# Staging the next expert's weights in dead attention buffers, with Pool copying them home, in a mixture-of-experts kernel

## Chip, cores and metric

The kernel runs on 1 core of one Trainium2 chip. The metric is the device time of one execution in microseconds (us); before the change the median of 3 runs is 1287.46 us (1286.85 to 1291.06).

The engines by their short names: PE is TensorE, DVE is VectorE, ACT is ScalarE, POOL is GpSimd, SP is SyncE, which here only issues DMAs.

## What is computed

One layer (float32, 256 latent tokens, 256 context tokens, width 1024): neighbourhood attention, a residual, then a mixture of experts over the 256 latent tokens, each token going to 4 of 32 experts. The experts' weights are 32 x (8 + 4) MiB = 403 MB and are read once.

```python
def moe(x, w_router, b_router, w_up, b_up, w_down, b_down):
    logits = (xt @ w_router + b_router).astype(jnp.float32)
    top_v, top_i = lax.top_k(logits, TOP_K)
    top_w = jax.nn.softmax(top_v, axis=-1)
    gates = jnp.sum(jax.nn.one_hot(top_i, N_EXPERTS, dtype=jnp.float32) * top_w[..., None], axis=1)
    for e in range(N_EXPERTS):
        hid = xt @ w_up[e] + b_up[e]
        x_glu = jnp.minimum(hid[:, :D_EXPERT], SWIGLU_LIMIT)
        x_lin = jnp.clip(hid[:, D_EXPERT:], -SWIGLU_LIMIT, SWIGLU_LIMIT)
        act = x_glu * jax.nn.sigmoid(SWIGLU_ALPHA * x_glu) * (x_lin + 1)
        y = act @ w_down[e] + b_down[e]
        out = out + gates[:, e:e + 1] * y.astype(jnp.float32)
```

The sub-layer ends with a norm, a gate and the residual.

## The kernel before

It is written engine by engine; every order is the program's own and all waits are on semaphores.

**The ring.** Weights of all stages pass through `ring`, 12 slots of 1 MiB. An expert is six chunks of 2 MiB, two slots each: chunks 0 to 3 hold `w_up` (two row blocks k of 128 each, 2048 columns: 1024 gated, 1024 linear), chunks 4 and 5 hold `w_down`. So the ring holds one expert, and each chunk has a fixed home. SP issues the chunks in order 0 to 5, expert by expert (`load_expert`, `expert`, L328 to L343). Before chunk j of expert e it waits until PE has released home j in the last block that uses expert e - 1 (`ring_free`, counted from the table `ends_i`). Expert 0's chunks are issued as the last attention weights are released; the table exists from `tables_ready` on (L887).

**Blocks.** Tokens of an expert are gathered 64 at a time into a block. An expert with more than 64 tokens takes two blocks on the same weights. This input has 35 blocks; block b + 1's tokens are gathered in the middle of block b.

**One block on PE** (`block_step`, L1190): the up products, 8 row blocks x 2 halves x 2 column groups (L1201), the two column groups running side by side; the bias from `bup_parts` (L1211); the sums of the first 128 tokens of the block before (`combine`, L1187: `combT` times `y`, two halves of 64 rows); two transposes of `comb` (L1223); the gather of the next block (L1127); `combine` of the other 128 tokens; transposes of `act` (L1233, L1237) and of the next tokens (L1135); the down products (L1248). PE releases a chunk after its last matmul on it.

**Beside it.** DVE clamps the gated and the linear part after the whole up half, multiplies (`act`, L905 to L915), adds the sums from PSUM into `acc` (L899) and makes `comb`, the 0/1 choice times the gate. ACT does the sigmoid, copies the gathered tokens, `combT`, half of `aT`, and `y` out of PSUM. POOL works in the attention part (scaling, L440; bias masks, L429) and takes inverse square roots (`powers`, L377); in the experts it has nothing to do until the end.

**Memory.** `tokens` holds inputs, then bias tables, then `bup` and `bdown`; `kT_mem` holds keys, then `x1` and `h2T`; `v_mem` holds values, then all small buffers of a block (`xT`, `glu`, `lin`, `sig`, `act`, `aT`, `y`, `combT`). Between attention and the experts: W_o products (L1091), ACT's squares (L544), DVE's split of `b_up` in three bfloat16 parts (L779 to L784), `gate2` (L789), two norms, the router and the ranks.

Of the kernel before, what the change touches and what calls it, by code (L numbers as in the profile page):

```python
# [18 lines left out]
BF16 = mybir.dt.bfloat16  # L19
# [4 lines left out]
P = 128  # L24
D = 1024
TOK = 256
# [16 lines left out]
PER, UPS = 6, 4  # L43
# [3 lines left out]
def build(nc, x, c, ctx_in, c_ctx, ada_w, ada_b, norm_g, w_qkv, w_o, rpb, w_router, b_router,  # L47
          w_up, b_up, w_down, b_down, out):
    with ExitStack() as st:
# [9 lines left out]
        def sem(name):  # L59
# [8 lines left out]
        tokens = sb("tokens", [P, 4, D])  # L68
        bias = tokens[:, :, :].rearrange("p a d -> p (a d)")[:, 0:BIAS_SLOTS * BIAS_ROWS * GRID_W].rearrange(
            "p (b c) -> p b c", c=BIAS_ROWS * GRID_W)  # L70
# [6 lines left out]
        kT_mem = sb("kT_mem", [P, KC * 512])  # L77
        kT = kT_mem[:, :].rearrange("p (k t) -> p k t", k=KC)
        x1 = kT_mem[:, 0:2048].rearrange("p (t d) -> p t d", t=2)
        h2T = kT_mem[:, 2048:4096].rearrange("p (k t) -> p k t", k=KC)  # L80
# [3 lines left out]
        v_mem = sb("v_mem", [P, 4 * D])  # L84
        v = v_mem[:, :].rearrange("p (t d) -> p t d", t=4)

        xT = v_mem[:, 0:512].rearrange("p (j s) -> p j s", j=4)
        glu = v_mem[:, 512:1024]
        lin = v_mem[:, 1024:1536]
        sig = v_mem[:, 1536:2048]  # L90
        act = v_mem[:, 2048:2560]
        aT = v_mem[:, 2560:3072].rearrange("p (j s) -> p j s", j=4)
        y = v_mem[:, 3072:3584]
        combT = v_mem[:, 3584:3840].rearrange("p (t s) -> p t s", t=2)
        tmp = v_mem[:, 0:2048].rearrange("p (t d) -> p t d", t=2)
        junk = v_mem[:, 2048:3072]
# [4 lines left out]
        gate1, shift2, scale2, gate2 = mod  # L101

# [6 lines left out]
        adab = sb("adab", [P, 3, HALF])  # L109
        rows = sb("rows", [P, HALF])  # L110
# [34 lines left out]
        bup = tokens[0:E, 0:2, :].rearrange("p a d -> p (a d)")  # L145
        xe = hT_mem[:, 0:HALF]
        bup_parts = tokens[:, 2, :].bitcast(BF16)[0:3 * E, :]
        bup_part = hT_mem[0:E, 2048:3072].bitcast(BF16)
        bdown = tokens[0:E, 3, :]
# [8 lines left out]
        block_no = sb("block_no", [E, NCOL])  # L158
        whose_i = sb("whose_i", [1, NCOL], I32)
# [28 lines left out]
        wo_done, x1_ready, h2_ready = sem("wo_done"), sem("x1_ready"), sem("h2_ready")  # L188
# [23 lines left out]
        def expert_chunk_here(eng, e, j):  # L212

            eng.wait_ge(expert_in[j], e * 16 + 16)
# [138 lines left out]
        def _(pool):  # L353
# [92 lines left out]
            for k in range(2, 6):  # L446
                powers(k, 1)
# [835 lines left out]
```

## Time and profile before

| | |
|---|---|
| median of 3 runs | 1287.46 us |
| profiled execution | 1288.93 us, its span 1287.2 us |
| PE busy | 1207.2 us, 94% of the span |
| DVE, ACT, POOL busy | 372.5, 185.8, 59.2 us |
| DMA | 454.40 MB, mean 353 GB/s |
| chain that ended last | PE 52%, DMA 39%, DVE 4% |
| mean granted TensorE clock | 0.985 of full |

The shares are means over the attention part (till about 271 us), the experts (277 to 1273) and the end. Matmul busy times are modelled; where the distance from one start to the next is given, it is the safer number. The chain that ended last names at each time what the next step waited for: that is the view that tells which resource sets the time of a stretch.

### The profile page before, as it was taken

Reading aid. Unit: us, or ns where it says so; the run is one execution under the profiler, and the core shown is the slowest. Engines: PE = TensorE matmul, PEld = TensorE weight load, DVE = VectorE, ACT = ScalarE, POOL = GpSimd, SP = SyncE. Lnnn points to the kernel's source line nnn. Section 1 sums busy time; section 2 is a strip of 40 time slices with the busy share of each in tenths; the row PEclk is TensorE's granted clock in tenths of the full one; section 3 lists DMA queues with packets and bytes.
Section 4 is the critical chain, followed back from the end, with each engine's and each line's share of the span. In section 5 each row is a group of like instructions: output and inputs, shape, how many; then the busy total and the mean of one; then the engine's idle time right before and its main releaser. Section 6 shows DMA issues by size and latency. Waiting matters only on the chain.

```text
span 1287.2 us, 15187 instructions
## 1 busy us (share of the span) xinstructions
PE 1207.2 (94%) x5850; PEld 536.9 (42%) x5851; DVE 372.5 (29%) x737; ACT 185.8 (14%) x360; POOL 59.2 (5%) x89
## 2 busy tenths in 40 slices
PE   5899999889999999999999999999999999999996
PEld 1888655453343433333333333333443333333342
DVE  1944364631321112222111111122211122211114
ACT  2200264110111001110010000011110011101001
POOL 2230053000000000000000000000000000000000
PEclk9899999979999999999999999999999999999998
DMA  9973488309499999999999999999699999999590
GB/s 372 369 208 131 160 258 318 130 27 383 184 415 429 430 428 429 427 429 430 428 429 427 429 430 428 429 428 403 256 416 429 429 427 429 428 428 429 238 391 33
DMA packets 49044, 454.40 MB, mean 353 GB/s; under 512 B 16736, under 2 KB 16776, under 8 KB 20320
## 3 DMA queue, kind: packets, MB, share of 16 engines
q1 hardware_dynamic: 48064, 450.90, 84.7%
q0 software_dynamic: 512, 1.72, 0.4%
q10 hardware_dynamic: 448, 1.50, 0.4%
q8 instruction: 13, 0.21, 0.1%
q14 instruction: 7, 0.06, 0.0%
HBM read 453.06 MB, written 1.05 MB: 353 GB/s over the span
## 4 chain that ended last, share of the span: by engine, by line
PE 52%; DMA 39%; DVE 4%; issue 2%; ACT 1%; SPq 0%; POOL 0%; DVEq 0%; POOLq 0%
DMA ring<-in_moe_w_up 37%; PE pair L1201 23%; PE pair L1248 9%; PE pair L1010 9%; PE pair L1091 2%; DMA ring<-in_ada_w 2%; PE pair L1187 1%; PE pair L1026 1%; PE pair L968 1%; DVE hT_mem L899 1%; PE pair L1036 1%; PE pair L1049 1%; DVE v_mem L905 1%; DVE v_mem L906 1%; PE pair L1135 1%
## 5 line engine op out<-in xcount | busy, mean ns | idle before, releaser
L1201 PE MATMUL pair<-ring,v_mem 128*64 128x512 f32 x2240 | 495.8, 594 | 29.6 <-DMA ring<-in_moe_w_up 29.2
L1201 PEld LDWEIGHTS pair<-ring,v_mem 128*64 128x64 f32 x2240 | 181.1, 137 | 336.0 <-issue 274.5
L1248 PE MATMUL pair<-ring,v_mem 128*64 128x512 f32 x1120 | 248.1, 595 | 1.5
L905 DVE TENSOR_SCALAR v_mem<-pair 128x512 f32<-128x512 f32 x35 | 24.2, 692 | 719.8 <-PE pair L1211 719.8
L1248 PEld LDWEIGHTS pair<-ring,v_mem 128*64 128x64 f32 x1120 | 92.5, 137 | 132.9 <-issue 132.7
L579 ACT ACTIVATE v_mem<-v_mem 128x512 f32<-128x512 f32 x35 | 22.1, 630 | 538.8 <-DVE v_mem L905 538.8
L899 DVE TENSOR_TENSOR hT_mem<-hT_mem,pair 128x512 f32<-128x512 f32 x140 | 89.4, 680 | 8.0 <-PE pair L1187 8.0
L1187 PE MATMUL pair<-v_mem 64*128 64x512 f32 x280 | 78.8, 641 | 3.4 <-ACT v_mem L591 0.8
L1127 PE MATMUL pair<-q_mem,pT_mem 128*64 128x512 f32 x288 | 71.5, 618 | 1.3 <-DVE pT_mem L848 1.3
L379 POOL TENSOR_TENSOR rstd<-ms,neghalf 128x1 f32<-128x1 f32 (+1 forms) x8 | 4.7, 594 | 1071.7 <-DVE ms L627 1071.7
L591 ACT ACTIVATE v_mem<-pair 128x512 f32<-128x512 f32 x35 | 20.9, 597 | 228.7 <-PE pair L1248 228.7
L1010 PE MATMUL pair<-mod_high,ring_low 128*128 128x256 f32 (+1 forms) x128 | 44.7, 349 | 4.7 <-DVE ring_low L691 4.6
L1187 PEld LDWEIGHTS pair<-v_mem 64*128 64x128 f32 x280 | 21.2, 185 | 48.7 <-DVE hT_mem L899 32.6
L968 PE MATMUL pair<-ring,condT 128*32 128x512 f32 x192 | 25.7, 663 | 9.4 <-DMA ring<-in_ada_w 9.4
L564 ACT ACTIVATE hT_mem<-pair 128x512 f32<-128x512 f32 x36 | 21.5, 597 | 77.7 <-PE pair L1127 77.7
L1127 PEld LDWEIGHTS pair<-q_mem,pT_mem 128*64 128x64 f32 x288 | 17.8, 138 | 28.5 <-issue 27.1
L1010 PEld LDWEIGHTS pair<-mod_high,ring_low 128*128 128x128 f32 x128 | 25.4, 198 | 8.2 <-DVE ring_low L691 5.7
L1091 PE MATMUL pair<-ring,hT_mem 128*128 128x512 f32 x64 | 27.7, 594 | 0.0
L909 DVE SCALAR_TENSOR_TENSOR v_mem<-v_mem 128x512 f32<-128x512 f32 x35 | 24.2, 692 | 3.7
L918 DVE COPY v_mem<-pair 128x256 f32<-128x256 f32 x35 | 14.9, 424 | 35.1 <-PE pair L1233 35.1
L1010 PE MATMUL pair<-ring_low,mod_high 128*128 128x512 f32 x64 | 24.9, 389 | 0.0
L915 DVE TENSOR_TENSOR v_mem<-v_mem 128x512 f32<-128x512 f32 x35 | 24.0, 686 | 0.0
(217 smaller groups left out, 944.5 us busy)
## 6 DMA issues: line engine op xcount, KB each, us to landing
ring<-in_moe_w_up SPq DMA_DIRECT2D x128, 2048.0 KB, 23.2
ring<-in_moe_w_down SPq DMA_DIRECT2D x64, 2048.0 KB, 20.3
ring<-in_ada_w SPq DMA_DIRECT2D x24, 1024.0 KB, 8.4
ring<-in_na_w_qkv SPq DMA_DIRECT2D x12, 1024.0 KB, 27.4
ring<-in_na_w_o SPq DMA_DIRECT2D x4, 1024.0 KB, 15.1
tokens<-in_na_rpb SPq DMA_DIRECT2D x32, 96.0 KB, 6.4
gain<-in_norm_g POOLq DMA_DIRECT2D x3, 512.0 KB, 5.7
tokens<-in_x SPq DMA_DIRECT2D x1, 1024.0 KB, 5.0
```

The costliest lines, as they stand in the source:

```text
L579: s.activation(sig, glu, ACT.Sigmoid, scale=ALPHA).then_inc(sig_ready, 1)
L899: d.tensor_tensor(dst, dst, bank[banks[n]][:, :], ALU.add).then_inc(acc_done, 1)
L905: d.tensor_scalar(glu, bank[0][:, :], LIMIT, None, ALU.min).then_inc(glu_ready, 1)
L909: d.scalar_tensor_tensor(act, lin, 1.0, glu, ALU.add, ALU.mult).then_inc(pre_ready, 1)
L915: d.tensor_tensor(act, act, sig, ALU.mult).then_inc(act_ready, 1)
L968: last = mm(bank[b][32 * j:32 * j + 32, :], condT[:, k, :], wchunk(n)[:, HALF * j:HALF * j + HALF], start=k == 0, stop=k == KC - 1)
L1010: last = mm(out_, left, right, start=k == 0 and part == 0, stop=k == KC - 1 and part == 2)
L1091: last = mm(bank[4 + 2 * t + i][:, :], oT[:, k, P * t:P * t + P], wpair(WO, k)[:, HALF * i:HALF * i + HALF], start=k == 0, stop=k == KC - 1)
L1127: last = mm(bank[3][64 * n:64 * n + 64, :], pick[:, t, :], h2[:, t, HALF * n:HALF * n + HALF], start=t == 0, stop=t == 1)
L1187: mm(bank[banks[n]][:, :], combT[64 * n:64 * n + 64, t, :], y[64 * n:64 * n + 64, :], start=True, stop=True).then_inc(part_done, 1)
L1201: last = mm(bank[half][64 * n:64 * n + 64, :], xT[:, k % 4, 64 * (k // 4):64 * (k // 4) + 64], w[:, c0:c0 + HALF], start=k == 0, stop=False)
L1248: last = mm(bank[2][64 * n:64 * n + 64, :], aT[:, j, 64 * half:64 * half + 64], w[:, HALF * n:HALF * n + HALF], start=k == 0, stop=k == KC ...
```

## The change

1. `kT_mem`, `tokens` and `v_mem` become one `zone` of six slots, three places of 2 MiB. Expert 1's chunks 0 to 2 are loaded there as soon as scores, bias tables and values are dead. From then on SP issues, for each e, chunks 3, 4, 5 of e to their homes and then chunks 0, 1, 2 of e + 1 to the zone.
2. POOL copies each staged chunk to its home, eight copies of 128x512, after the home is released; PE waits for `staged[j]` instead of the DMA for chunks 0 to 2, and SP waits for it before reusing the place.
3. The small buffers of a block move to `hT_mem` and to dead modulation buffers; some now share memory (`glu` with `xe`, `lin` with `act`), which adds waits of ACT for `act_ready` and `sig_ready`. `bup`, `bup_parts`, `bdown`, `x1`, `junk` move; `gate2` is made before the split of `b_up`, ACT's squares wait for the split, and the load of `b_down` is issued later in ACT's chain.
4. In the last up chunk PE finishes the gated half with its bias first (`glu_done`), then the linear half. DVE clamps and multiplies by the sigmoid in between.
5. The sums: `comb` holds only 0 and 1; `y` is scaled by the slot's gate on its way out of PSUM and split into `y_high` and `y_low`, so that `combT` and both parts are one-pass operands: eight one-pass matmuls a block instead of four. The gates per slot come from two more matmuls with one column.

The diff, cut to its core:

```diff
+        zone = sb("zone", [P, ZONE, 2048])
+        kT_mem = zone[:, 0:2, :].rearrange("p s n -> p (s n)")
+        token_mem = zone[:, 2:4, :].rearrange("p s n -> p (s n)")
+        v_mem = zone[:, 4:6, :].rearrange("p s n -> p (s n)")
...
         def expert_chunk_here(eng, e, j):
 
-            eng.wait_ge(expert_in[j], e * 16 + 16)
+            if j < STAGED:
+                eng.wait_ge(staged[j], e + 1)
+            else:
+                eng.wait_ge(expert_in[j], e * 16 + 16)
...
+            for j in range(4):
+                sp.wait_ge(ring_free, EXP - RING + 2 * j + 2)
+                load_expert(0, j, expert_chunk(j))
+            sp.wait_ge(s_done, DUOS)
+            sp.wait_ge(expert_in[0], 16)
+            load_expert(1, 0, staged_chunk(0))
+            sp.wait_ge(bias_used, DUOS)
+            sp.wait_ge(expert_in[1], 16)
+            load_expert(1, 1, staged_chunk(1))
+            sp.wait_ge(o_done, DUOS)
+            sp.wait_ge(expert_in[2], 16)
+            load_expert(1, 2, staged_chunk(2))
+            for j in range(4, PER):
+                sp.wait_ge(ring_free, EXP - RING + 2 * j + 2)
+                load_expert(0, j, expert_chunk(j))
+
+            def second_half(e):
+
+                blocks_before = sp.value_load(ends_i[0:1, bass.ds(e - 1, 1)], min_val=1, max_val=E + MAX_EXTRA)
+                for j in range(STAGED, PER):
                     sp.wait_ge(ring_free, blocks_before * PER + (EXP - PER + j + 1))
-                    load_expert(e, j)
+                    load_expert(e, j, expert_chunk(j))
+
             sp.wait_ge(tables_ready, 1)
+            with sp.Fori(1, E - 1) as e:
+                second_half(e)
+                for j in range(STAGED):
+                    sp.wait_ge(staged[j], e + 1)
+                    load_expert(e + 1, j, staged_chunk(j))
+            second_half(E - 1)
...
+            pool.wait_ge(tables_ready, 1)
+            with pool.Fori(1, E) as e:
+                blocks_before = pool.value_load(ends_i[0:1, bass.ds(e - 1, 1)], min_val=1, max_val=E + MAX_EXTRA)
+                for j in range(STAGED):
+                    pool.wait_ge(expert_in[j], e * 16 + 16)
+                    pool.wait_ge(staged[j], e)
+                    pool.wait_ge(home_free[j], e)
+                    pool.wait_ge(ring_free, blocks_before * PER + (EXP - PER + j + 1))
+                    mark = staged_mark[:, j:j + 1]
+                    g.tensor_tensor(home_mark[:, j:j + 1], mark, mark, ALU.add).then_inc(home_free[j], 1)
+                    for i in range(8):
+                        c = slice(HALF * i, HALF * i + HALF)
+                        last = g.tensor_copy(expert_chunk(j)[:, c], staged_chunk(j)[:, c])
+                    last.then_inc(staged[j], 1)
             powers(6, 1)
             powers(7, 1)
...
-            sc.wait_ge(s_done, DUOS)
+            sc.wait_ge(o_done, DUOS)
+            sc.dma_start(bup, b_up[0]).then_inc(in_bup, 16)
+            sc.wait_ge(bc_done, 8)
             sc.dma_start(x1, token_rows(x)).then_inc(in_res, 16)
-            sc.wait_ge(bias_used, DUOS)
-            sc.dma_start(bup, b_up[0]).then_inc(in_bup, 16)
-            sc.dma_start(bdown, b_down[0]).then_inc(in_bdown, 16)
+            sc.wait_ge(bup_split, 1)
...
                 sc.wait_ge(gather_done, b + 1)
+                if not isinstance(b, int) or b > 0:
+                    sc.wait_ge(act_ready, b)
+                    sc.wait_ge(sig_ready, b)
                 s.activation(xe, bank[3][:, :], ACT.Copy).then_inc(xe_ready, 1)
...
                     sc.wait_ge(part_done, b * 4 + 4)
+                s.activation(gate_slot, bank[4][:, TOK:TOK + 1], ACT.Copy).then_inc(slot_gates, 1)
                 s.activation(combT, bank[4][:, 0:TOK].rearrange("p (t s) -> p t s", t=2), ACT.Copy).then_inc(combT_ready, 1)
...
-                s.activation(y, bank[2][:, :], ACT.Copy).then_inc(y_ready, 1)
+                sc.wait_ge(slot_gates, b + 1)
+                s.activation(y_high, bank[2][:, :], ACT.Copy, scale=gate_slot).then_inc(y_ready, 1)
...
+                ve.wait_ge(glu_done, b + 1)
+                d.tensor_scalar(glu, bank[0][:, :], LIMIT, None, ALU.min).then_inc(glu_ready, 1)
+                ve.wait_ge(glu_ready, b + 1)
+                ve.wait_ge(sig_ready, b + 1)
+                d.tensor_tensor(glu, glu, sig, ALU.mult).then_inc(pre_ready, 1)
                 ve.wait_ge(up_done, b + 1)
...
+                d.scalar_tensor_tensor(act, lin, 1.0, glu, ALU.add, ALU.mult).then_inc(act_ready, 1)
...
+                ve.wait_ge(y_ready, b + 1)
+                d.scalar_tensor_tensor(y_low, bank[2][:, :], gate_slot, y_high, ALU.mult, ALU.subtract).then_inc(y_split, 1)
...
                 for n in range(2):
-                    mm(bank[banks[n]][:, :], combT[64 * n:64 * n + 64, t, :], y[64 * n:64 * n + 64, :],
-                       start=True, stop=True).then_inc(part_done, 1)
+                    mm(bank[banks[n]][:, :], combT[64 * n:64 * n + 64, t, :], y_high[64 * n:64 * n + 64, :],
+                       start=True, stop=False)
+                for n in range(2):
+                    mm(bank[banks[n]][:, :], combT[64 * n:64 * n + 64, t, :], y_low[64 * n:64 * n + 64, :],
+                       start=False, stop=True).then_inc(part_done, 1)
...
+                expert_chunk_here(pe, e, UPS - 1)
                 pe.wait_ge(bsel_ready, b + 1)
+                up(0, KC - 2)
+                up(0, KC - 1)
+                add_bias(0).then_inc(glu_done, 1)
+                up(1, KC - 2)
+                up(1, KC - 1).then_inc(ring_free, 1)
+                add_bias(1).then_inc(up_done, 1)
```

## Rows read from the trace of the kernel before

**Rows 1.** page, part 2: moved GB/s, 40 slices of 32.18 us, numbered from 0
```profile
GB/s 372 369 208 131 160 258 318 130 27 383 184 415 429 430 428 429 427 429 430 428 429 427 429 430 428 429 428 403 256 416 429 429 427 429 428 428 429 238 391 33
```

**Rows 2.** chain that ended last, in order of time: start us, us, what
```profile
509.76 3.68 PE pair L1201 x16
...
891.50 3.65 PE pair L1201 x16
...
1059.12 24.43 DMA ring<-in_moe_w_up
...
1201.06 3.65 PE pair L1201 x16
```

**Rows 3.** busy us by stretch; granted clock, DMA share and GB/s come last
```profile
560.00:800.00 240.00, 225.04 (x1032) 82.93 (x1030) 50.67 (x112) 25.53 (x48) 0.00 (x0) 1.00 1.01 429
901.00:912.00 11.00, 10.96 (x55) 4.64 (x56) 2.03 (x6) 1.58 (x3) 0.00 (x0) 1.00 0.00 0
```

**Rows 4.** timeline of SP, 905 to 940: start us, us, engine, line, operation
```profile
912.33 10.63 SPq L331 DMA_DIRECT2D ring<-in_moe_w_up  x4
932.75 3.77 SPq L331 DMA_DIRECT2D ring<-in_moe_w_down  x2
```

**Rows 5.** timeline of all engines, one block, 349 to 377
```profile
348.97 1.13 PE L1187 MATMUL pair<-v_mem 64*128 64x512 f32 x4
...
349.08 0.69 DVE L905 TENSOR_SCALAR v_mem<-pair 128x512 f32<-128x512 f32 x1 [19.90 <-PE pair L1211]
...
351.08 1.28 DVE L899 TENSOR_TENSOR hT_mem<-hT_mem,pair 128x512 f32<-128x512 f32 x2
...
352.41 1.13 PE L1187 MATMUL pair<-v_mem 64*128 64x512 f32 x4
...
353.47 0.51 PE L1233 MATMUL pair<-ident,v_mem 128*128 128x128 f32 x2
...
353.62 0.38 ACT L585 ACTIVATE v_mem<-pair 128x256 f32<-128x256 f32 x1 [0.64 <-PE pair L1187]
...
355.08 7.09 PE L1248 MATMUL pair<-ring,v_mem 128*64 128x512 f32 x32
...
376.27 1.13 PE L1187 MATMUL pair<-v_mem 64*128 64x512 f32 x4
```

**Rows 6.** groups of Pool by form: count, busy us, mean ns, idle
```profile
L440 POOL TENSOR_SCALAR mod<-mod,rinv 128x512 f32<-128x512 f32 x32 | 21.7, 691 | 38.1 <-DVE rinv L749 38.1
...
L398 POOL TENSOR_SCALAR qcol<-qcol 128x1 f32<-128x1 f32 x1 | 0.3, 260 | 0.1
...
L356 POOL MEMSET ones<- 128x128 f32 x1 | 0.2, 204 | 0.3 <-POOLq L1273 0.3
```

**Rows 7.** timeline of PE, 138 to 142 and then 284 to 286
```profile
138.01 0.39 PE L1010 MATMUL pair<-gain_high,mod_high 128*128 128x512 f32 x1
138.24 0.39 PE L1010 MATMUL pair<-gain_high,hT_low 128*128 128x512 f32 x1
...
284.25 0.42 PE L1165 MATMUL pair<-mod 32*128 32x48 f32 x2
284.51 0.38 PE L1166 MATMUL pair<-mod,ones 32*128 32x48 f32 x2
```

**Rows 8.** timeline before the experts, 205 to 310
```profile
221.34 0.44 ACTq L534 DMA_DIRECT2D tokens<-in_moe_b_down  x1
...
226.15 1.22 DVE L779 CAST tokens<-tokens 32x2048 bf16<-32x2048 f32 x1 [1.70 <-DMA tokens<-in_moe_b_up]
...
235.22 1.29 DVE L789 TENSOR_TENSOR mod<-pair,gain 128x512 f32<-128x512 f32 x2
...
242.91 1.28 DVE L810 SCALAR_TENSOR_TENSOR q_mem<-q_mem,rstd,mod 128x1024 f32<-128x1024 f32 x1 [0.68 <-POOL rstd L379]
...
250.57 1.04 PE L1105 MATMUL pair<-ident,q_mem 128*128 128x128 f32 x8
```

**Rows 9.** timeline of the end, 1264 to 1287
```profile
1272.91 0.60 ACT L591 ACTIVATE v_mem<-pair 128x512 f32<-128x512 f32 x1 [6.53 <-PE pair L1248]
```

More of the change, by code:

```diff
@@ L83, in build @@
         h2 = q_mem[:, :].rearrange("p (t d) -> p t d", t=2)
[L84 to L96, printed above, removed]
+        v = v_mem.rearrange("p (t d) -> p t d", t=4)
+        tmp = acc
+        last_tmp = v_mem[:, 0:2048].rearrange("p (t d) -> p t d", t=2)
+        last_junk = v_mem[:, 2048:3072]
         mod_high, mod = [], []
@@ L144, in build @@
         br = sb("br", [P, E])
[L145 to L149, printed above, removed]
+        junk = pT_mem[:, :]
+        bup = hT_mem[0:E, 2048:4096]
+        bup_parts = gain[:, :].bitcast(BF16)[0:3 * E, :]
+        bup_part = pT_mem[0:E, :].bitcast(BF16)
+        bdown = mod[0][0:E, :]
         rank_e, gate_e2 = small[:, 0:2, :], small[:, 4:6, :]
@@ L188, in build @@
         wo_done, x1_ready, h2_ready = sem("wo_done"), sem("x1_ready"), sem("h2_ready")
+        staged = [sem(f"staged{j}") for j in range(STAGED)]
+        home_free = [sem(f"home_free{j}") for j in range(STAGED)]
         h2T_done, h2T_ready, logit_done = sem("h2T_done"), sem("h2T_ready"), sem("logit_done")
@@ L776, in _ @@
                 d.scalar_tensor_tensor(scale2[:, h], bank[i][:, :], 1.0, gain[:, h], ALU.add, ALU.mult).then_inc(bc_dve, 1)
+            ve.wait_ge(in_gain, 48)
+            for i in range(2):
+                ve.wait_ge(bc_done, 6 + i + 1)
+                h = slice(HALF * i, HALF * i + HALF)
+                d.tensor_tensor(gate2[:, h], bank[2 + i][:, :], gain[:, h], ALU.mult).then_inc(bc_dve, 1)
+            ve.wait_ge(bc_dve, 6)
             ve.wait_ge(in_bup, 16)
@@ L784, in _ @@
             d.tensor_copy(bup_parts[2 * E:3 * E, :], bup).then_inc(bup_split, 1)
-            ve.wait_ge(in_gain, 48)
-            for i in range(2):
-                ve.wait_ge(bc_done, 6 + i + 1)
-                h = slice(HALF * i, HALF * i + HALF)
-                d.tensor_tensor(gate2[:, h], bank[2 + i][:, :], gain[:, h], ALU.mult).then_inc(bc_dve, 1)
             ve.wait_ge(in_res, 16)
@@ L1206, in block_step @@
                         make_tables()
+                expert_chunk_here(pe, e, UPS - 1)
                 pe.wait_ge(bsel_ready, b + 1)
-                for half in range(2):
-                    for n in range(2):
-                        c0 = D * half + HALF * n
-                        last = mm(bank[half][64 * n:64 * n + 64, :], bsel, bup_parts[:, c0:c0 + HALF],
-                                  start=False, stop=True)
-                last.then_inc(up_done, 1)
+                up(0, KC - 2)
[4 more added lines that the diff above has]
+                add_bias(1).then_inc(up_done, 1)
                 if is_first:
@@ L1222, in block_step @@
                 for t in range(2):
-                    last = tr(bank[4][:, P * t:P * t + P], comb[:, t, :, :].rearrange("p a s -> p (a s)"), ident[:, :])
+                    tr(bank[4][:, P * t:P * t + P], comb[:, t, :, :].rearrange("p a s -> p (a s)"), ident[:, :])
+                for t in range(2):
+                    last = mm(bank[4][:, TOK:TOK + 1], comb[:, t, :, :].rearrange("p a s -> p (a s)"), gate_tok[:, t:t + 1],
+                              start=t == 0, stop=t == 1)
                 last.then_inc(combT_done, 1)
```

101 lines of the change are left out of this document (57 added, 44 removed).

## The prediction

> **What bounds the kernel now.** I read the page's rates over time first, then the chain that ended last in order of time, then the timelines. The rates [rows 1] show three things: an attention part with gaps in the DMA, a long flat plateau near 429 GB/s, and dips in slices 28 and 37 (from 0). The chain [rows 2] says what the plateau is: from 509.76 to 891.50, and again from 1059.12 to 1201.06, it is the DMA of an expert's up chunk followed by TensorE (PE) working that chunk, one turn per expert. (891.50 - 509.76)/13 = 29.36 us, for 12.58 MB: 429 GB/s at a DMA share of 1.01 [rows 3]. There the transfer itself is the limit and PE waits for it. Before 509 and from 891.50 to 1059 PE is the limit: one block takes 376.27 - 348.97 = 27.30 us [rows 5], less than 29.36.
>
> What gives PE the arrears it then works off is an expert with more than 64 tokens: two blocks on the same weights. Experts 1, 20 and 30 are such. At expert 20, chunk 3 lands at 891.50 [rows 2], the DMA idles from 901 to 912 [rows 3], and SP issues four loads from 912.33 and the down loads at 932.75 [rows 4], each when the second block has finished that buffer; (10.63 - 0.33)/3 = 3.43 us is thus PE's time for one chunk.
>
> **The staged chunks.** Three changes in sequence. The stream of chunks was 0,1,2,3,4,5 of expert e, then 0 of e+1; it stays in that order, only 0,1,2 may now be issued before their home is free. So in the plateau nothing is gained: the DMA is full already. At a two-block expert the three go out in the 11 us of idle time. But the next in the stream, chunks 3, 4 and 5, still go home. Chunk 4 is released by the second block's down half at 932.75, before as after. Old: chunks 0 to 3 from 912.33 are nearly through by then (912 to 933 is about four transfers of 29.36/6 = 4.89 us). New: 0 to 2 are through at 916, 3 goes when released at 912.33 + 10.3 = 922.6, is through at about 930, and the DMA waits for 932.75. From there on the same chunks flow in the same order at the same rate. The idle time has moved, not shrunk: gain 0. The same at expert 1, where PE is the limit, and at the start, where block 0 has its weights.
>
> The cost: each staged chunk passes Pool, eight copies of 128x512. No row has such a copy. Nearest: a one-input TENSOR_SCALAR of the same shape, 691 ns; with one column 260 ns, so 0.84 ns a column; a MEMSET of 128x128 takes 204 ns [rows 6], of which 128 columns at that slope are 107, so 97 are fixed and 512 columns would take 0.53 us. A copy lies between 0.53 and 0.69; I take 0.62, nearer the row that also reads. With the tiny marking add and waits (0.25 assumed, from the 260 ns row) a chunk takes 8 x 0.62 + 0.25 = 5.21 us, a little over the 4.89 in which it lands. In the plateau, count from the landing of chunk 3 at 0. Chunk 0 landed at -14.7; Pool ends chunk 2 at -14.7 + 0.1 + 3 x 5.21 = +1.0; PE works chunk 2 until 4.5 and only then chunk 3, which it used to begin at 0.05. So PE runs 4.45 us later against the DMA stream. This costs no period, since 3 x 5.21 = 15.6 < 29.36, and it is paid once on entering each DMA-bound stretch. At the two-block expert that ends the stretch, PE's lag becomes lag of the stream (its release at 932.75 comes 4.45 later). Two stretches end so, at experts 20 and 30: 2 x 4.45 = 8.9 us. Bounds: at 0.53 a chunk takes 4.5, Pool keeps up, the lag is one copy plus one chunk of PE less 4.89, 3.1 us, total 6.2; at 0.69 it is 3 x 5.77 - 14.6 + 3.4 = 6.2, total 12.3.
>
> A rule weighed here. The GpSimd page (GPSIMD Engine Reference, 3.1 and 4.1 of the Trainium skill) calls one-input work about line rate, but gives 768 ns for 512 elements of a loop with more operations; as an estimate by that page the loss would be 16 us in place of 8.9. The 691 ns row is below its figure, and the row decides.
>
> **The block of PE.** After the change the block matters only where PE releases the stream: a mid and a second block at experts 1, 20, 30, and the last. Counted along the chain that is 7 block lengths, so a change d of the block is worth 7d. Old, from the end of the up half: sums at 348.97, two transposes and the gather until 352.41, sums until 353.47 (1.06), transposes, down at 355.08: 6.11 us [rows 5].
> - One-pass sums: a pass of 512 columns is issued each 0.227 us [rows 7]. Two row halves run together in the old 1.06 (two passes of 3.43/8 = 0.43, plus 0.2). New: 2 x 0.227 + 0.2 = 0.66, a gain of 0.8 for both; if the halves don't run together, 1.12, a loss of 0.1.
> - Two more matmuls for the gates, one column wide, 128x128 weights. The small ones at full clock are issued 0.26 apart [rows 7]; two, their weights loading partly ahead: +0.45. Bounds 0.25 and 0.9.
> - ScalarE (ACT) now copies the gates (about 0.2, an estimate: half of the 0.38 that combT takes for 256 columns [rows 5]) ahead of combT, which starts 0.15 after the second sums (353.62 against 353.47). PE's high transposes wait for it: +0.4.
> - Gated half first: VectorE (DVE) starts when two pairs and a bias, 1.96 us, are still to come; five steps of up to 0.69 [rows 5] and their gaps, 3.65, have act ready 1.7 us after the up half instead of 4.0, and the two running sums after it end at 3.0. The second sums, old just after them (DVE from 351.08, two of 0.64, PE 352.41 [rows 5]), come at 3.5. Cover 0.5 us. The extra DVE subtract runs beside the next up half.
> Sum: -0.8 + 0.45 + 0.4 - 0.1 for the rest is 0 or so: d = 0, bounds -0.8 and +1.0, or -5.6 and +7 us in all.
>
> The Trainium skill (SBUF — State Buffer, Who interferes with whom) has a rule against this change: VectorE and GpSimd share a port pair under an exclusive lock, and a Vector instruction with two SBUF inputs waits out a GpSimd instruction that reads. No row here has the two side by side. It is a rival below.
>
> **Start and end.** The b_up split now needs gate2 first, and ACT's squares wait for it. Old: split from 226.15, gate2 at 235.22, so 9.1 us; second-norm of half 0 ended at 244.2 (242.91 + 1.28), with PE busy on W_o until 250.57 [rows 8]. New: gate2 cannot begin before its gain (issued after the scale, some 6 us with staged loads in the queue) at about 231; split to 242; norm at 251: cover 6.4 us, used up. ACT also issues the b_down load in its chain, 0.44 us [rows 8]. I take +0.5, bounds 0 and +4 (staged loads crowding x, b_up and the gain). What is queued behind: SP now stands at o_done with the last two chunks of expert 0 behind it, which are not due before 247. Pool's powers come before its copies; those of expert 1 start with the tables at 287.5 and take 16 us, block 1 begins at 307.5: hidden. End: y needs ACT 0.60 [rows 9] and DVE 0.69 in place of ACT alone, and the first sums are shorter by 0.4: +0.3.
>
> Sum: 8.9 + 0 + 0.5 + 0.3 = 9.7 us. The profiled execution took 1288.93 (span 1287.2), the median is 1287.46; 1288.93 + 9.7 = 1298.6, by the median 1297.2. I predict 1297.
>
> **The rivals.**
> - Forecast, 1291 to 1306 with its bounds: 0.60.
> - Faster: the staged loads really fill the idle 11 us at experts 20 and 30, because PE is after that not held by chunks 4 and 5. It would give 1287.5 - 22 + 9.7 = 1275. For it: the idle is there [rows 3]. Against it: 932.75 [rows 4]. It decides once 5 us of each idle stretch are saved, since 2 x 5 outweighs 9.7. 0.08.
> - No change: copies at 0.53 and a block shorter by 0.8 give 6.2 - 5.6 + 0.8, about +1.4: 1289. 0.14.
> - The block gets longer: Pool's copies hold DVE's two SBUF-to-SBUF products by up to 0.6 each, the cover of 0.5 is gone, and the row halves don't overlap: d = +1.0, 1305; with copies of 0.69, 1309, and with a slow start 1313. 0.10.
> - Pool slower: at 0.85 a copy the lag is 3 x 7.05 - 14.6 + 3.4 = 10 per stretch, +20: 1308; at 1.0 the copies begin to hold the next loads as well and it is over 1320. 0.08.
>
> Range 1284 to 1314: below it lies the faster case, above it the slow Pool's greater part and what I haven't seen. About 0.3% (3.9 us) is what a measurement of this kernel can tell from no change. Faster by more: 0.09; within: 0.13; slower by more: 0.78.
>
> **What the new profile would show.** Pool copies of 0.53 to 0.69 us, 744 of them (24 for each of 31 experts); PE in the plateau waiting at up chunks 0 to 2 for Pool, no longer at chunk 3 for the DMA; the plateau's period still 29.36 and starting two to three experts earlier; at expert 20 two idle stretches of the DMA in place of one, together about 11 us, and the down load issued some 4 to 5 us later than 932.75; one-pass sums of 0.66 a pair. I am wrong if a DMA-bound period is below 29.3, if the idle at the two-block experts is much below 11 us, or if PE's block is under 26 us.

## The result and the profile after

| | before | after |
|---|---|---|
| median | 1287.15 us (4 runs) | 1452.98 us (4 runs, 1450.01 to 1457.16) |
| profiled execution, its span | 1288.93, 1287.2 us | 1453.33, 1451.6 us |
| mean granted TensorE clock | 0.985 | 0.91 |
| DVE busy | 372.5 us | 687.1 us |
| POOL busy | 59.2 us | 493.2 us |

The ratio is 1.128, 95% interval 1.126 to 1.131: the change makes the kernel 13% slower. I had predicted 1297 us with a range of 1284 to 1314. The direction was right; the size is off by a factor of 17 (165.8 us for a predicted 9.7), so a mechanism is missing in the sum.

The page of after, part 2, has the granted clock and the moved GB/s in 40 slices, here of 36.3 us (before: [rows 1]):

```profile
PEclk9999999689999888899999999989999999988998
...
GB/s 378 301 224 112 202 361 279 57 99 249 268 381 377 374 372 366 347 369 381 378 375 375 371 395 383 377 376 324 125 379 377 375 372 393 382 377 374 313 140 62
```

The flat plateau near 429 is gone: 366 to 395 nearly everywhere. The DMA no longer sets the period of an expert. The groups of instructions by line, PE, POOL and DVE (count, busy us, mean ns, idle before them):

```profile
L496 POOL COPY ring<-zone 128x512 f32<-128x512 f32 x744 | 417.6, 603 | 0.0
L1328 PE MATMUL pair<-ring,mod 128*64 128x512 f32 x1120 | 311.5, 719 | 25.1 <-DVE mod L976 25.0
...
L970 DVE SCALAR_TENSOR_TENSOR hT_mem<-hT_mem 128x512 f32<-128x512 f32 x35 | 123.9, 3540 | 3.7
L912 DVE TENSOR_SCALAR pT_mem<-slot_no,rank_col 128x128 f32<-128x128 f32 x70 | 98.9, 1454 | 0.0
L917 DVE CAST mod<-mod 96x64 bf16 (+1 forms) x36 | 93.9, 2609 | 0.0
```

L970 is the product that makes `act`, 128x512 with two SBUF inputs. Before, the same product (L909) took 0.69 us; now 3.54. L917 is the cast of `bsel` to bfloat16, 0.18 us of work, and L912 makes `comb`: both write SBUF from SBUF with one input. None has become larger. The timeline of all engines in one block, from the end of the up half (start us, us, engine, line; before: [rows 5]):

```profile
666.98 0.50 PE L1247 MATMUL pair<-mod_high 64*128 64x512 f32 x2
...
667.44 4.49 POOL L496 COPY ring<-zone 128x512 f32<-128x512 f32 x8
...
668.01 4.47 DVE L970 SCALAR_TENSOR_TENSOR hT_mem<-hT_mem 128x512 f32<-128x512 f32 x1
...
672.40 1.27 DVE L956 TENSOR_TENSOR hT_mem<-hT_mem,pair 128x512 f32<-128x512 f32 x2
672.47 4.49 POOL L496 COPY ring<-zone 128x512 f32<-128x512 f32 x8
...
673.60 3.42 DVE L917 CAST mod<-mod 96x64 bf16 x1
673.73 0.52 PE L1247 MATMUL pair<-mod_high 64*128 64x512 f32 x2 [3.45 <-DVE hT_mem L956]
...
676.93 0.41 DVE L976 COPY mod<-pair 128x256 f32<-128x256 f32 x1
...
677.23 4.49 POOL L496 COPY ring<-zone 128x512 f32<-128x512 f32 x8
...
677.39 8.81 PE L1328 MATMUL pair<-ring,mod 128*64 128x512 f32 x32 [0.60 <-DVE mod L976]
```

POOL starts its first row of eight copies at 667.44, as the staged chunk 0 has landed (its marking add before the row had waited 18.17 us for that DMA), and this falls just on the end of an up half. DVE's product starts 0.57 us later and ends 0.55 us after the row (672.48 against 671.93). So DVE does not wait for one piece of 0.56 us, but for all eight. This block is no exception: 27 of the 35 products take 4.3 us or more. The adds from PSUM (L956) run beside the second row unharmed, 1.27 us for two; the cast is caught and ends, at 677.02, with that row (676.96). PE stands 3.45 us for the adds (3.3 to 3.5 us in the 27 blocks), and its down half waits for DVE's copy of `aT` (L976) behind the cast. From the end of the up half to the down half is 677.39 - 666.98 = 10.41 us; it was 6.11 [rows 5].

The busy time by stretch (PE, PEld, DVE, ACT, POOL; then granted clock, DMA share, GB/s; before: [rows 3]):

```profile
560.00:760.00 200.00, 173.91 (x774) 62.41 (x772) 102.32 (x96) 20.06 (x42) 84.06 (x162) 0.90 0.90 374
...
674.00:677.40 3.40, 2.80 (x13) 1.50 (x12) 3.40 (x3) 1.40 (x4) 3.26 (x8) 0.51 1.02 439
677.40:681.00 3.60, 3.60 (x10) 1.13 (x12) 3.60 (x3) 0.03 (x1) 3.60 (x7) 0.51 0.88 373
```

After PE has stood 3.45 us, its granted clock is 0.51, the lower level (1.2 GHz), until about 681 (1.00 from 681 to 684). This stretches the down half from 7.1 to 8.81 us; over the blocks it takes 7.1 to 9.7. All down halves together take 311.5 us; 35 at 7.09 would be 248. A period, from one down half to the next, is 32.4 to 34.1 us where the product is held, above the DMA's 29.36 [rows 2, 3]. So two effects are to be told apart, the hold on DVE and the clock, and both from the mere traffic of the copies.

### The profile page after: what moved, and what is told of

The parts are those of the page before. It is cut to its first block, busy times and chain, and to the rows that moved or that the text cites. A ratio compares the mean times of both kernels' runs of the same rounds, so it can differ in the third digit from the quotient of the medians.

```text
span 1451.6 us, 16852 instructions
## 1 busy us (share of the span) xinstructions
PE 1267.8 (87%) x5990; PEld 542.5 (37%) x5991; DVE 687.1 (47%) x808; ACT 191.0 (13%) x395; POOL 493.2 (34%) x933
## 4 chain that ended last, share of the span: by engine, by line
PE 67%; DVE 14%; issue 12%; DMA 3%; ACT 2%; DVEq 0%; POOL 0%; SPq 0%; POOLq 0%; ACTq 0%
PE pair L1261 29%; PE pair L1328 21%; PE pair L1070 8%; DVE hT_mem L965 3%; DVE hT_mem L956 3%; DVE mod L917 3%; DMA ring<-in_ada_w 2%; DVE hT_mem L962 2%; ACT hT_mem L634 1%; DVE hT_mem L967 1%; PE pair L1086 1%; PE pair L1028 1%; PE pair L1096 1%; DMA gain<-in_norm_g 1%; PE pair L1109 1%
## 5 line engine op out<-in xcount | busy, mean ns | idle before, releaser
L1261 PE MATMUL pair<-ring,hT_mem 128*64 128x512 f32 x2240 | 492.8, 592 | 0.3 <-issue 0.3
L496 POOL COPY ring<-zone 128x512 f32<-128x512 f32 x744 | 417.6, 603 | 0.0
L1328 PE MATMUL pair<-ring,mod 128*64 128x512 f32 x1120 | 311.5, 719 | 25.1 <-DVE mod L976 25.0
L1261 PEld LDWEIGHTS pair<-ring,hT_mem 128*64 128x64 f32 x2240 | 160.6, 137 | 312.8 <-issue 310.1
L1328 PEld LDWEIGHTS pair<-ring,mod 128*64 128x64 f32 x1120 | 93.2, 166 | 224.9 <-issue 189.7
L970 DVE SCALAR_TENSOR_TENSOR hT_mem<-hT_mem 128x512 f32<-128x512 f32 x35 | 123.9, 3540 | 3.7
L1247 PE MATMUL pair<-mod_high 64*128 64x512 f32 x140 | 36.3, 516 | 101.6 <-DVE hT_mem L956 99.9
L912 DVE TENSOR_SCALAR pT_mem<-slot_no,rank_col 128x128 f32<-128x128 f32 x70 | 98.9, 1454 | 0.0
L917 DVE CAST mod<-mod 96x64 bf16 (+1 forms) x36 | 93.9, 2609 | 0.0
L956 DVE TENSOR_TENSOR hT_mem<-hT_mem,pair 128x512 f32<-128x512 f32 x140 | 89.0, 674 | 0.9 <-PE pair L1250 0.9
L965 DVE TENSOR_TENSOR hT_mem<-hT_mem 128x512 f32<-128x512 f32 x35 | 43.2, 1234 | 26.8 <-ACT hT_mem L634 26.8
```

The costliest lines, as they stand in the source:

```text
L496: last = g.tensor_copy(expert_chunk(j)[:, c], staged_chunk(j)[:, c])
L912: d.tensor_scalar(comb[:, t, :, :], slot_no[:, :, :], ranks[:, t, bass.ds(b, 1)], None, ALU.is_equal)
L917: d.tensor_copy(bsel, owner3[:, bass.ds(b, 1)].to_broadcast([3 * E, SLOTS])).then_inc(bsel_ready, 1)
L956: d.tensor_tensor(dst, dst, bank[banks[n]][:, :], ALU.add).then_inc(acc_done, 1)
L965: d.tensor_tensor(glu, glu, sig, ALU.mult).then_inc(pre_ready, 1)
L970: d.scalar_tensor_tensor(act, lin, 1.0, glu, ALU.add, ALU.mult).then_inc(act_ready, 1)
```

## The experiments

**e1_eighth: seven of eight copies taken away.** It stages, waits and marks as the changed kernel does.

```diff
-                    for i in range(8):
+                    for i in range(1):
```

> The changed kernel, but Pool copies only the first 512 of each staged chunk's 4096 columns; seven eighths of the up weights of chunks 0 to 2 are left out. All waits, marks and the order of the DMAs stay. Theory A (DVE instructions stand behind Pool's uninterrupted row of eight copies, PE behind DVE): no DVE instruction waits more than about 0.6 us, PE's block falls from 33 to 34 us to 26.8 to 27.4, the plateau is DMA-bound again at 29.36 us, and the time is 1287 + 6 (start) - 7 x 0.5 (shorter block) = 1290, within 5. Theory B (the staging itself costs: waits of SP on Pool, order of the DMAs, mark instructions): the period stays above 31 and the time above 1350.

Measured: 1289.19 us, ratio 1.0013 (1.0002 to 1.0023). L970 takes 0.69 us, L917 and L912 are back, the plateau has 29.36 us a period. The copies are the cause of all but a few us. SP's issues at expert 20 (timeline of SP) judge the step on the idle time:

```profile
926.96 0.34 SPq L346 DMA_DIRECT2D ring<-in_moe_w_up  x1
936.31 3.77 SPq L346 DMA_DIRECT2D ring<-in_moe_w_down  x2
```

Chunk 3 goes when its home is released and the down loads 9.35 us later; they went at 932.75 [rows 4]. Staging starts nothing earlier there, even without the cost of the copies.

**e2_memset: the home is written, the staged chunk is not read.**

```diff
-                        last = g.tensor_copy(expert_chunk(j)[:, c], staged_chunk(j)[:, c])
+                        last = g.memset(expert_chunk(j)[:, c], 0.0)
```

> Each of Pool's copies becomes a memset of the same 128x512 of the home; Pool writes and reads nothing, so the up weights of chunks 0 to 2 are zeros (left out). Some 0.53 us each. If any Pool work holds DVE: L970 (two SBUF inputs), L912 and L917 (one SBUF input) stay at 3 to 4 us, the time 1430 to 1450. If only the read interface is shared: L970 falls to 0.7, and also L912 and L917 fall, time 1290 to 1300. If two-input instructions collide on reads and one-input ones on writes: L970 0.7, L912 and L917 still up to 3 us, time between, some 1320 to 1400.

Measured: 1294.97 us, 1.0054 (1.0034 to 1.0075). A row of eight takes 3.78 us, against 4.49 for the copies. Its timeline, POOL and DVE, in two places:

```profile
382.41 3.78 POOL L496 MEMSET ring<- 128x512 f32 x8
...
383.06 0.69 DVE L970 SCALAR_TENSOR_TENSOR hT_mem<-hT_mem 128x512 f32<-128x512 f32 x1
...
384.86 1.38 DVE L917 CAST mod<-mod 96x64 bf16 x1
...
421.58 3.77 POOL L496 MEMSET ring<- 128x512 f32 x8
...
422.86 2.58 DVE L906 TENSOR_SCALAR pT_mem<-slot_no,rank_col 128x64 f32<-128x64 f32 x2
```

The two-input product starts 0.65 us into a row that only writes, and is not held: 0.69 us, and so it is for all six of these products that lie beside memsets. The one-input cast, 1.8 us later, is held until the row ends (386.24 against 386.19), and so are the two picks (L906), 2.58 us for 0.4. So there are two conflicts here: the product with two SBUF inputs is held by copies, which read, and not by memsets; the one-input cast and TENSOR_SCALAR from SBUF to SBUF are held by both. The holds are those of the third expectation, the time that of the second: only three casts are held in this run, so its time doesn't tell what holding the cast alone would cost in every block. This is what the Trainium skill says (SBUF — State Buffer, Who interferes with whom): DVE's second input passes through an interface shared with GpSimd, and casts, copies and `tensor_scalar` may enter a mode that takes both shared ports. The trace agrees on both kinds: 0.69 against 4.47 us for the product, 1.38 in place of 0.18 for the cast beside a row that only writes.

**e3_gaps: the same copies, but POOL waits for the completion of each piece and adds one element before the next.**

```diff
                         last = g.tensor_copy(expert_chunk(j)[:, c], staged_chunk(j)[:, c])
+                        if i < 7:
+                            last.then_inc(piece_done, 1)
+                            pool.wait_ge(piece_done, e * 21 + (7 * j + i - 20))
+                            g.tensor_tensor(gap_mark[:, 0:1], mark, mark, ALU.add)
```

> All copies stay, but between two of the eight pieces Pool waits for the completion of the piece before it and does a one-element add. If the port is given anew at each gap, a DVE instruction waits for one piece at most (up to 0.6 us): PE's block 27 to 28 us, plateau at 29.36, but Pool's chunk takes about 8 x 0.85 = 7 us and PE's lag on entering each DMA-bound stretch is 3 x 7 - 14.6 + 3.4 = 10 us: time 1290 + 20 = 1310, within 8. If Pool keeps the port whatever the gap, or takes it again first: 33 us and more a block, over 1440.

Measured: 1311.35 us, 1.0182 (1.0161 to 1.0202). All 744 copies are there, each 0.60 us. The timeline, with DVE let in between two pieces (the product is L976 here):

```profile
356.54 0.18 POOL L502 TENSOR_TENSOR gap_mark<-staged_mark 1x1 f32<-1x1 f32 x1
356.57 1.25 DVE L976 SCALAR_TENSOR_TENSOR hT_mem<-hT_mem 128x512 f32<-128x512 f32 x1
356.67 0.60 POOL L498 COPY ring<-zone 128x512 f32<-128x512 f32 x1
...
357.35 0.52 POOL L502 TENSOR_TENSOR gap_mark<-staged_mark 1x1 f32<-1x1 f32 x1
```

The product waits out one piece (1.25 us), then POOL's next instruction waits for it (0.52 in place of 0.18). The mean of the product is 0.88 us. This is what I had priced in the prediction ("by up to 0.6 each"); it is true of pieces with a completed gap between them, and false of pieces issued back to back. At expert 20, SP issues chunk 3 at 937.15, 10.2 us later than e1_eighth: the slower copying (6.4 us a chunk, 345.09 to 351.45, in place of 0.7) is lag twice, 20.4 us, and 1289.2 + 20.4 = 1309.6 is nearly all of the time.

**e4_whole: one copy of 128x4096 per chunk.**

```diff
-                    for i in range(8):
-                        c = slice(HALF * i, HALF * i + HALF)
-                        last = g.tensor_copy(expert_chunk(j)[:, c], staged_chunk(j)[:, c])
+                    last = g.tensor_copy(expert_chunk(j), staged_chunk(j))
```

> The changed kernel with each staged chunk copied by one instruction of 128x4096 in place of eight of 128x512. If a DVE instruction stands behind Pool's whole uninterrupted row anyway, the eight pieces bought nothing: L970 stays near 4 us, the period near 34 us, the time within 1% of the changed kernel's 1453 (somewhat shorter, by seven fixed parts of some 0.1 us a chunk). If the pieces did let DVE in between, this one is slower, 1480 or more.

Measured: 1374.77 us, 1.0674 (1.0653 to 1.0696), outside both expectations. The groups by line:

```profile
L494 POOL COPY ring<-zone 128x4096 f32<-128x4096 f32 x93 | 333.7, 3588 | 0.0
L1326 PE MATMUL pair<-ring,mod 128*64 128x512 f32 x1120 | 274.4, 646 | 22.8 <-DVE mod L974 22.5
...
L968 DVE SCALAR_TENSOR_TENSOR hT_mem<-hT_mem 128x512 f32<-128x512 f32 x35 | 100.5, 2871 | 3.7
```

DVE does wait the whole of it out, as expected. But I had forgotten that the whole is shorter: 3.59 us in place of 4.49, so eight pieces pay (4.49 - 3.59)/7 = 0.13 us for each further instruction. The hold shrinks by 0.9, PE's wait with it, from 3.3 to 3.5 us down to 2.4 to 2.7, and 21 of the 35 down halves are at full clock again (7.09 us, the others 7.8 to 9.7): together 274.4 us in place of 311.5, so 37 of the 78 us gained are the down half. Cutting the copy in pieces, without a gap between them, made the hold longer, not shorter.

**e8_busy: PE is given 14 one-pass matmuls, into a bank that nobody reads, in the place where it waits.** Hold and copies stay.

```diff
                 else:
+                    for _ in range(14):
+                        mm(bank[5][:, :], combT[0:64, 0, :], y_high[0:64, :], start=True, stop=True)
                     combine(1, b)
```

> Edit: in every block PE issues 14 more one-pass matmuls of 512 columns (0.227 us each, 3.2 us) into a bank nobody reads, just where it waits 3.45 us for VectorE in the changed kernel. The wait itself and the copies stay. Theory A (the idle 3.45 us make TensorE's granted clock fall to 0.51, and that costs 1.7 us in the down half and 1.4 us before it): the down half is 7.1 us in nearly all blocks, the granted clock stays at 1.0, some 31 blocks are 3.1 us shorter, some 3 blocks without a wait are 3.2 us longer: 1453 - 96 + 10 = 1367, within 15. Theory B (the down half is slow because GpSimd copies into and reads the memory beside it, or because of anything that goes with the copies): down halves stay at 8 to 9.6 us, and the time is 1453 to 1465.

Measured: 1416.08 us, 1.1000 (1.0978 to 1.1022): faster than the changed kernel by 37 us for doing more. The stretch 560 to 760, and the timeline of PE and DVE in a block:

```profile
560.00:760.00 200.00, 189.29 (x908) 79.53 (x906) 113.06 (x104) 22.08 (x47) 94.37 (x182) 1.00 0.96 400
```

```profile
620.36 0.50 PE L1247 MATMUL pair<-mod_high 64*128 64x512 f32 x2
...
623.60 3.48 PE L1310 MATMUL pair<-mod_high 64*128 64x512 f32 x14
...
630.25 0.41 DVE L976 COPY mod<-pair 128x256 f32<-128x256 f32 x1
...
630.71 7.09 PE L1330 MATMUL pair<-ring,mod 128*64 128x512 f32 x32 [1.38 <-DVE mod L976]
```

The clock is 1.00 in place of 0.90 and the down half 7.09, and so are 28 of the 35. So in these blocks it was PE's standing that lowered the clock, not the copies: the third row of copies lies beside this down half too. The size was a miss (1367 expected). I had counted 1.4 us a block for the slow transposes ahead of the down half; but 630.71 - 620.36 = 10.35 us is what it was with the slow clock (10.41), since DVE's copy of `aT`, behind the held cast, ends it in both. What is left, from the starts of PE's groups in both traces: down halves together 260.0 us in place of 311.5, -51.5; the 34 stretches from an up half to the next down half 342.3 in place of 329.6, +12.7, of which 10.7 in the seven blocks where the product isn't held. That is -38.8, and the spans of the two profiled executions differ by 38.8 (1412.8 against 1451.6). Seven down halves still take 8.8 to 8.9 us. Six of them are ordinary held blocks, ahead of which PE stands only the 1.4 us for `aT`, as ahead of all the others; why the clock falls in these isn't settled.

**e9_after_dve: all copies back to back as in the changed kernel, but POOL waits once per expert until DVE has copied its half of `aT`.**

```diff
+                    if j == 0:
+                        pool.wait_ge(aT_dve, blocks_before)
```

> Edit: all 744 full copies stay; GpSimd waits once per expert, before the first staged chunk, until VectorE has copied its half of aT in the last block of the expert before (the instruction that PE's down half waits for). So no copy can stand beside VectorE's work between an up half and a down half; all of the copies lie beside the down half and the next up half. Theory A (only the hold on VectorE there costs): TensorE's block is back at 26.8 us; the two-input product is 0.69 us; in stretches where TensorE is the limit the three rows (14 us) end as TensorE needs the third chunk (7.1 + 2 x 3.43 = 14.0 us after the down half starts), so at most some 0.1 us a block. Against the eighth (1289.2, which has the same start and no row of copies to wait for) there is only the lag of one copied chunk on entering each of the two DMA-bound stretches, 3.3 us each: 1289.2 + 6.6 = 1296, within 5. Theory B (the copying itself costs, by its traffic beside TensorE's and the DMA's, or by what it does to VectorE beside the down half): over 1320.

Measured: 1295.26 us, 1.0061 (1.0044 to 1.0078); 1296 was expected. First the window 430 to 880, then the groups of DVE, then one piece of the timeline, then SP at expert 20:

```profile
430.00:880.00 450.00, 416.48 (x2012) 161.17 (x2009) 154.82 (x250) 52.46 (x111) 207.90 (x405) 1.00 1.01 429
```

```profile
L914 DVE TENSOR_SCALAR pT_mem<-slot_no,rank_col 128x128 f32<-128x128 f32 x70 | 124.5, 1820 | 0.0
...
L972 DVE SCALAR_TENSOR_TENSOR hT_mem<-hT_mem 128x512 f32<-128x512 f32 x35 | 24.2, 692 | 3.7
```

```profile
391.71 9.27 DVE L914 TENSOR_SCALAR pT_mem<-slot_no,rank_col 128x128 f32<-128x128 f32 x1
...
930.30 0.34 SPq L346 DMA_DIRECT2D ring<-in_moe_w_up  x1
939.65 3.77 SPq L346 DMA_DIRECT2D ring<-in_moe_w_down  x2
```

One wait gives back 158 us. The plateau is there again at 429 GB/s, and POOL copies as much as before. DVE is held longer than ever in one place, 9.27 us for an instruction of 0.28, through two whole rows (391.81 to 396.30 and 396.40 to 400.89); but this `comb` is not due until the next block's middle, and costs nothing. PE now waits for POOL's chunks, 44 times and 46.4 us in total, only where the DMA is the limit, as the prediction said it would. So neither the copying nor the hold costs the time, but the place of the hold, between the up and the down half. The issue at 930.30 is 3.34 us later than e1_eighth's, which is the lag of a copied chunk: 1289.2 + 2 x 3.34 = 1295.9.

**e5_unstaged: the staging is undone, all else kept** (new small buffers, gated half first, one-pass sums, the moved loads). SP loads all six chunks home, POOL has no copies.

```diff
-            if j < STAGED:
-                eng.wait_ge(staged[j], e + 1)
-            else:
-                eng.wait_ge(expert_in[j], e * 16 + 16)
+            eng.wait_ge(expert_in[j], e * 16 + 16)
...
+            for j in range(PER):
+                sp.wait_ge(ring_free, EXP - RING + 2 * j + 2)
+                load_expert(0, j, expert_chunk(j))
+            sp.wait_ge(tables_ready, 1)
+            with sp.Fori(1, E) as e:
+                blocks_before = sp.value_load(ends_i[0:1, bass.ds(e - 1, 1)], min_val=1, max_val=E + MAX_EXTRA)
+                expert(e, blocks_before)
```

> The changed kernel with its staging undone: every chunk goes home in the old order and Pool copies nothing; new memory layout, gated half first and one-pass sums stay. Theory A: block 26.8 us (the last block of the changed kernel, which has no copies beside it), plateau 29.36, time 1287.2 - 7 x 0.5 + 0.5 = 1284, within 3. If the one-pass sums or the new waits of ACT cost something in the long run, 1290 or more.

Measured: 1283.62 us, 0.9973 (0.9963 to 0.9983). These parts alone gain 3.8 us: seven block lengths at 26.76 in place of 27.30 us [rows 5] are 7 x 0.54 = 3.8.

**e6_nine: what staging would need.** The zone becomes places 6 to 8 of a ring of nine chunks of 2 MiB: no copy, any chunk goes to any place in turn, PE's code stands three times, for experts e mod 3. **e7_nine_late** is the same, with SP waiting for the norm gain and x before the first load into the zone (the last two lines of the edit).

```diff
-            s = (EXP + 2 * j) % RING
-            return ring[:, s:s + 2, :].rearrange("p s n -> p (s n)")
+            s = 2 * ((j + 2) % 9)
+            place = ring[:, s:s + 2, :] if s < RING else zone[:, s - RING:s - RING + 2, :]
+            return place.rearrange("p s n -> p (s n)")
...
             sp.wait_ge(s_done, DUOS)
+            sp.wait_ge(in_gain, 48)
+            sp.wait_ge(in_res, 16)
```

> The changed kernel with no copies: the three dead buffers become places 6 to 8 of a ring of nine chunks, chunk i of the stream always lies in place (i + 2) mod 9, PE runs each kind of expert (e mod 3) from its own code. SP loads chunk i once chunk i - 9 is released. Theory: what made staging worthless was that chunks 3 to 5 kept their only home; here the idle time of a two-block expert is filled by three chunks more of any kind. From the rows of before: DMA-bound stretches begin 3 x 4.89/2.6 = 5 to 6 experts later at a block of 26.76 us, time some 24 us under the unstaged 1283.6, less 6 for the slow start that the early loads give: 1255 to 1268. Rival (the two-block idle is set by PE, not by the number of places): 1283 to 1292.

> The kernel of nine places, but SP issues the first load into a dead attention buffer only once the last norm gain and x have landed. Theory on the start (the early loads delay the gain, gate2, the b_up split and so the router by 6 to 7 us): block 0 starts at 276 to 277 instead of 282 to 283, the time 5 to 7 us under that of the kernel of nine places. Rival (the delay is the new order of gate2 and split): no difference, within 1 us.

Measured: 1263.2 us, 0.9810 (0.9794 to 0.9827), and 1257.75 us, 0.9764 (0.9748 to 0.9780): 5.45 us less. Of e7_nine_late, the stretch 345 to 1200 by busy time:

```profile
345.00:1200.00 855.00, 830.28 (x4044) 346.07 (x4042) 221.23 (x496) 103.62 (x217) 0.00 (x0) 1.00 1.01 428
```

The DMA is full throughout this stretch: the idle stretches at experts 20 and 30, which the staging only split, are gone. The time is 30 us, 2.4%, below the kernel before; against e5_unstaged, which has the same shorter block, the ring of nine gains 26. The later start of the loads is seen where DVE waits for the gain (timeline of e7_nine_late; in after the same line, L839, has 13.99 in place of 6.45):

```profile
232.57 1.29 DVE L822 TENSOR_TENSOR mod<-pair,gain 128x512 f32<-128x512 f32 x2 [6.45 <-DMA gain<-in_norm_g]
```

## Why the prediction was wrong, step by step

**The staged chunks gain nothing: right.** After, too, the DMA idles twice at expert 20; these are SP's issues there (timeline of SP; [rows 4] before):

```profile
989.91 1.37 SPq L346 DMA_DIRECT2D zone<-in_moe_w_up  x3
1030.04 0.34 SPq L346 DMA_DIRECT2D ring<-in_moe_w_up  x1
1045.00 3.77 SPq L346 DMA_DIRECT2D ring<-in_moe_w_down  x2
```

But with PE as the limit everywhere, the length of that idle time says nothing. e1_eighth, whose DMA is the limit again, is the test (busy time by stretch; [rows 3] before):

```profile
920.00:930.00 10.00, 10.00 (x54) 4.10 (x50) 3.97 (x7) 0.63 (x1) 1.23 (x3) 1.00 0.22 56
930.00:940.00 10.00, 9.83 (x50) 4.58 (x50) 2.09 (x6) 2.41 (x6) 0.00 (x0) 1.00 0.63 239
```

The DMA share is 0.22 and 0.63 there, 11.5 us of idle time in two parts; e5_unstaged, without staging, has 0.09 from 898 to 911, 11.8 us in one. And the profiled span of e1_eighth is longer by 7.2 us (1288.5 against 1281.3), of which 7.07 are there when block 0 begins (283.39 against 276.33). From there on the staging itself gains and costs next to nothing.

My point of decision was right as well: chunks 3 to 5 still need their own homes. e6_nine frees them of it, and gains.

**A copy of 128x512 at 0.62 us: right.** 0.603 us alone, 0.56 in a row. The row of eight is 4.49 us and the chunk with its mark 4.6, under the 4.89 in which it lands, so the lower of my two cases holds. **The lag**, predicted 4.45 per DMA-bound stretch with a lower bound of 3.1, is 3.34 (e9_after_dve): 6.7 in place of 8.9 us. (My upper bound, 3 x 5.77 - 14.6 + 3.4, is 6.1 and not 6.2.)

**The block, d = 0: the mean was fair, what surrounds it failed.** Without copies beside it, as in the last block of after (timeline of PE; [rows 5]), it is:

```profile
1424.19 0.50 PE L1247 MATMUL pair<-mod_high 64*128 64x512 f32 x2
...
1427.43 0.50 PE L1247 MATMUL pair<-mod_high 64*128 64x512 f32 x2
...
1428.10 0.51 PE L1313 MATMUL pair<-ident,hT_mem 128*128 128x128 f32 x2
...
1429.76 2.79 PE L1328 MATMUL pair<-ring,mod 128*64 128x512 f32 x12
```

The sums take 1428.10 - 1427.43 = 0.67 us in place of 1.06, as priced (0.66). What I had charged at 0.4 for ACT's copy of the gates is 0.05: from the transposes of `act` to the down half it takes 1.66 us, and took 1.61. The rest of the middle is shorter by 0.2 in spite of the gate matmuls. So d is 5.57 - 6.11 = -0.54, within my bounds, and 7d = -3.8 us.

**The step that failed** is the rival "Pool's copies hold DVE's two SBUF-to-SBUF products by up to 0.6 each", which I gave 0.10 and +1.0 a block. The mechanism was the right one and its size was wrong in four ways, each of which a run shows:

1. The unit of the hold is not a piece but the uninterrupted row: 4.47 us, not 0.6. The copies beside block 0, which I had called hidden, are no exception: its first product (L965) is held 9.33 us, through the rest of one row and the whole of the next. e3_gaps puts a completed gap between the same pieces and gets 0.88.
2. It also takes one-input work. I priced only the products; the cast of `bsel`, an instruction of 0.18 us that I never mentioned, is held 3.4 us and stands ahead of the `aT` copy for which PE's down half waits. The sentence that I cited from the Trainium skill (SBUF — State Buffer, Who interferes with whom) covers the product, and speaks of the length of one GpSimd instruction, where the measured hold lasts for the row; the same section names casts and `tensor_scalar`, and I didn't weigh that half. e2_memset separates the two kinds.
3. It makes PE stand 3.45 us a block, after which its granted clock is at the lower level, 0.51 to 681. The down half shown pays 1.7 us, all of them 63.4, of which e8_busy gives back 51.5. I had no term for the clock.
4. The multiplier was 7 block lengths, since only there PE releases the stream. With 32 to 34 us a block PE is the limit everywhere, and every held block pays. A price for a block is worth 7d only as long as 27.30 + d stays below 29.36, that is up to d = 2.06 at most; beyond it each block counts.

Together: after against e9_after_dve, the same copies elsewhere, is 1452.98 - 1295.26 = 158 us. The view of the waits has for after (us in total, times, longest us):

```profile
PE pair L1247 <- DVE hT_mem L956: 99.9, 30, 3.5
...
PE pair L1328 <- DVE mod L976: 25.0, 27, 1.3
```

The starts of PE's groups in the two traces give the whole sum. The 34 stretches from an up half to the next down half take 329.6 us in place of 189.3, +140.3: these waits, and the small matmuls at the lower clock (in the block shown transposes take 0.70 in place of 0.51 and 1.06 in place of 0.64). The down halves are 311.5 - 248.1 = 63.4 longer. Block 0 takes 8.0 more to its down half. In exchange the up halves are 56.2 shorter, since PE no longer waits in them for the DMA and for POOL. With 0.9 for the later start of block 0 that is 156.4 us; the spans of the profiled executions differ by 156.6 (1451.6 against 1295.0).

**The start, +0.5: too low, and out of its bounds.** From PE's first W_o product to block 0 it took 276.94 - 223.07 = 53.9 us before; after (the chain that ended last, in order of time):

```profile
224.46 13.67 DMA gain<-in_norm_g
...
282.77 1.47 PE pair L1261 x5
```

With W_o begun at 222.72 that is 60.05 us, 6.2 more. I had named the cause ("staged loads crowding x, b_up and the gain") and capped it at +4, with the gain landing 6 us after its issue; it took 13.67, since three staged loads of 2 MiB had been issued from 212.30 on. Without staging it is 54.1 (e5_unstaged, 276.33 - 222.27), and so it is with the loads held back: e7_nine_late, 278.86 - 224.75 = 54.1, against 59.6 of e6_nine.

**Had the hold been absent**, the forecast would have stood: lag +6.7, block -3.8, start +6.2 give 1287.4 + 9.1 = 1296.5; e9_after_dve measures 1295.26, and I had written 1297. That is partly luck: my 8.9, 0 and 0.5 were each off by 2 to 6 us and cancelled. The range failed because the rival with the unmeasured resource was bounded by the size of a piece, for which no row spoke.

## What to carry to other kernels

Before GpSimd gets bulk work in SBUF, list every DVE instruction that may lie beside it, the smallest ones too, and price each as held for the whole uninterrupted row, then ask who waits for that instruction: the cure here was not smaller pieces but one wait that moves the row to where DVE's results are not due. When a price per block could lift the block over the other resource's period, the count of blocks in the sum changes from the few to all of them. And if a buffer is free but the data must end elsewhere, first ask whether the consumer can read it where it lands: the ring of nine does without a copy and is 2.4% faster than the kernel before, 0.3% of it from the shorter block.

## What the runs showed of the hardware

- Back-to-back GpSimd instructions keep DVE out from the first to the last: 4.47 us beside a row of 4.49, and 9.27 us through two rows with a one-element add between them (e9_after_dve). A wait for the completion of each piece lets DVE in (e3_gaps).
- A row that only writes holds a one-input cast (until the row ends, 1.38 us in place of 0.18) and not a two-input product (0.69).
- Adds with one input in PSUM, 128x512, are not held: the mean of the 140 is 0.674 to 0.680 us in every kernel.
- A GpSimd copy of 128x4096 takes 3.59 us, eight of 128x512 take 4.49.
- After standing 3.45 us TensorE had a granted clock of 0.51 for about 7 us; after 2.4 to 2.7 us (e4_whole) 14 of the 35 down halves were slow. PE filled with matmuls of no use kept 1.00 in 28 of the 35 (e8_busy).
- A 512 KiB load from GpSimd's queue, issued behind three loads of 2 MiB from SP's, took 13.67 us to land; the same load takes 3.9 us in the kernel before, without them.
